# Latent attention in another order of query blocks: 7, 0, 6, 1, 5, 2, 4, 3 in place of 7 down to 0

## The reference, cut to what matters

```
logits = q_h . k_lat * 256**-0.5   (+ a large negative number where hidden)
p      = softmax(logits)           over keys of blocks 0..i for query block i
o_h    = p . (k_lat[64:] w_uv_h)   the values of each head, made before
```

## Time and profile before

| | |
|---|---|
| time, median of 3 runs | 2830.73 us (2829.38 to 2832.75) |
| the profiled execution's own time, and its span | 2828.45 us, 2826.6 us |
| TensorE busy over the span | 2685.5 us (95%) |
| VectorE, ScalarE, GpSimd busy | 1899.6 (67%), 1090.0 (39%), 1674.9 us (59%) |
| latent attention, first score product to the last weighted values | 1793.3 to 2091.1 us |

### The profile page before, as it was taken

How to read it: one execution, slowest core, us unless ns; L and a number is a source line. 1 busy time by engine, 2 the same in 40 slices (tenths; PEclk the granted TensorE clock), 3 DMA queues, 4 the chain that set the end, 5 groups by cost and what they waited for, 6 DMA issues and landing times.

```text
span 2826.6 us, 42358 instructions
## 1 busy us (share of the span) xinstructions
PE 2685.5 (95%) x15781; PEld 1357.9 (48%) x16048; DVE 1899.6 (67%) x2637; ACT 1090.0 (39%) x1665; POOL 1674.9 (59%) x916
## 2 busy tenths in 40 slices
PE   7999888999999999999899999888999999999998
PEld 4666554454444444444444444455554444444443
DVE  6888778575666674256999999777747656664043
ACT  3566566243333200014554343677743433331000
POOL 4777656336677679845348777711113566675884
PEclk9999999999999999999999999999999999999999
DMA  4122455631111153332213222598873111113332
GB/s 150 50 64 72 95 117 120 192 119 54 60 54 55 63 179 127 105 132 82 53 38 149 104 82 97 126 193 193 193 216 130 68 60 60 60 54 126 127 105 97
DMA packets 312622, 297.98 MB, mean 105 GB/s; under 512 B 252720, under 2 KB 252848, under 8 KB 312480
## 3 DMA queue, kind: packets, MB, share of 16 engines
q1 hardware_dynamic: 300672, 272.05, 33.6%
q10 hardware_dynamic: 11808, 23.99, 2.6%
HBM read 189.51 MB, written 35.70 MB: 80 GB/s over the span
## 4 chain that ended last, share of the span: by engine, by line
PE 78%; DVE 6%; issue 4%; DMA 4%; ACT 3%; POOL 2%; ACTq 1%; DVEq 0%; POOLq 0%; SPq 0%
PE ps L1684 23%; PE ps L327 20%; PE ps L309 14%; PE ps L2501 4%; DMA pt<-split 4%; PE ps L643 4%; PE ps L392 4%; PE ps L913 2%; PE ps L2012 2%; PE ps L649 1%; PE ps L2056 1%; DVE split L841 1%; PE ps L884 1%; PE ps L2518 1%; DVE prob L1028 1%
## 5 line engine op out<-in xcount | busy, mean ns | idle before, releaser
L266 POOL TENSOR_TENSOR w_hi<-w_stage,ones 128x1024 bf16<-128x1024 f32 (+1 forms) x115 | 237.6, 2066 | 139.7 <-PE ps L327 85.3
L269 POOL TENSOR_TENSOR w_lo<-w_stage,w_hi 128x1024 bf16<-128x1024 f32 (+1 forms) x115 | 266.5, 2317 | 9.0
L1501 DVE SCALAR_TENSOR_TENSOR x_res<-x_res,ps 128x1024 f32<-128x1024 f32 x32 | 39.0, 1218 | 319.6 <-PE ps L327 318.8
L327 PE MATMUL ps<-w_hi,hid_hi 128*128 128x512 bf16 x689 | 206.3, 379 | 1.6 <-POOL w_lo L269 0.8
L327 PE MATMUL ps<-w_hi,hid_lo 128*128 128x512 bf16 x690 | 206.5, 379 | 0.7
L327 PE MATMUL ps<-w_lo,hid_hi 128*128 128x512 bf16 x690 | 206.5, 379 | 0.7
L2501 PE MATMUL ps<-lat_hi,q_now 128*128 128x512 bf16 (+3 forms) x737 | 186.3, 325 | 5.5 <-DVE row_max L2566 5.5
L309 PE MATMUL ps<-xt_hi,w_hi 128*128 128x512 bf16 x598 | 178.8, 379 | 3.1 <-DVE score L2171 2.5
L309 PE MATMUL ps<-xt_hi,w_lo 128*128 128x512 bf16 x596 | 178.3, 379 | 0.6
L309 PE MATMUL ps<-xt_lo,w_hi 128*128 128x512 bf16 x592 | 177.6, 379 | 0.8
L1684 PE MATMUL ps<-xt_lo,w_hi 128*128 128x512 bf16 x426 | 161.6, 379 | 0.5
(11 more groups left out here) (305 smaller groups left out, 7513.8 us busy)
## 6 DMA issues: line engine op xcount, KB each, us to landing
w_stage<-in_l_up SPq DMA_DIRECT2D x88, 512.0 KB, 3.8
w_stage<-in_l_down SPq DMA_DIRECT2D x88, 512.0 KB, 3.7
w_stage<-in_l_o SPq DMA_DIRECT2D x32, 512.0 KB, 5.9
w_stage<-in_l_q SPq DMA_DIRECT2D x32, 512.0 KB, 5.4
q_split<-q_out SPq DMA_DIRECT2D x32, 512.0 KB, 2.6
q_now<-q_split SPq DMA_DIRECT2D x16, 1024.0 KB, 5.4
w_stage<-in_l_qkv SPq DMA_DIRECT2D x24, 512.0 KB, 4.1
x_spilled<-x_res ACTq DMA_DIRECT2D x16, 512.0 KB, 2.6
```

The costliest lines, as they stand in the source:

```text
L266: pool.tensor_tensor(hi, w_stage[slot][:, 0:cols], ones[:, 0:1].to_broadcast([P, cols]), ALU.mult).then_inc(w_cast[slot], 1)
L269: pool.tensor_tensor(lo, w_stage[slot][:, 0:cols], hi, ALU.subtract).then_inc(w_split[slot], 1)
L327: mm = pe.matmul(ps[:, bank + h, :], a[:, k, rows], w[:, h * HALF:(h + 1) * HALF], start=(k == first and m == 0), stop=(k == tiles - 1 and ...
```

## The change

`latent_block(t)` takes the place of `query_block(t)` everywhere in this stage. A head's steps then have 8, 1, 7, 2, 6, 3, 5 and 4 key blocks. The lags, the waits, the buffers, the number of instructions and the elements that each handles stay. A group of four steps now holds blocks 7, 0, 6, 1 or 5, 2, 4, 3, so that the reciprocal, the scaling and the context's parts address two runs of two blocks in place of one run of four. The pair's two query loads stay ahead of steps 6 and 14, which are now steps of 5 key blocks, followed by one of 4 (before: of 2, followed by one of 1).

```diff
+LATENT_ORDER = (7, 0, 6, 1, 5, 2, 4, 3)
+
+
+def latent_block(t):
+    return LATENT_ORDER[t % TB]
...
-            i = query_block(t)
+            i = latent_block(t)
             pair = split7[t % 4][:, 0:i + 1, :, :]
...
-            cols = slice(HALF, SEQ) if t == 11 else slice(0, HALF)
-            return xt_hi[:, pair, cols], xt_lo[:, pair, cols], ps[:, quad_bank(t), :]
+            twos, _ = quad(t)
+            hi, lo = [x[:, pair, :].rearrange("p (a n) -> p a n", a=4)[:, twos, :] for x in (xt_hi, xt_lo)]
+            return hi, lo, ps[:, quad_bank(t), :].rearrange("p (a n) -> p a n", a=2)
...
-            i = query_block(t)
-            return slice(i, i + 4), t // 8
+            first, second = sorted({latent_block(t - n) // 2 for n in range(4)})
+            return slice(first, second + 1, second - first), t // 8
+
+        def in_twos(ap):
+
+            return ap.rearrange("p (a b) -> p a b", b=2)
...
-                    t, i, hh = slot, query_block(slot), slot // 8
+                    t, i, hh = slot, latent_block(slot), slot // 8
...
-                    blocks, _ = quad(t)
+                    blocks = sorted(latent_block(t - n) for n in range(4))
                     pe.wait_ge(t_cx, 4 * p + t // 4 + 1)
-                    for q, b in enumerate(range(blocks.start, blocks.stop)):
+                    for q, b in enumerate(blocks):
...
-                    blocks, hh = quad(t)
+                    twos, hh = quad(t)
+                    inverse = in_twos(inv7[:, hh, :])[:, twos, :]
                     dve.wait_ge(t_pv, STEPS * p + t + 1)
-                    dve.reciprocal(inv7[:, hh, blocks], sum7[:, hh, blocks]).then_inc(t_ri, 1)
+                    dve.reciprocal(inverse, in_twos(sum7[:, hh, :])[:, twos, :]).then_inc(t_ri, 1)
...
-                m = query_block(t) + 1
+                m = latent_block(t) + 1
                 wait_if(sp, t_pv, STEPS * pair + t - 3)
```

More of the change, by code:

```diff
@@ L2505, in latent_tensor @@
                 if t is not None:
-                    i, hh = query_block(t), t // 8
+                    i, hh = latent_block(t), t // 8
                     if prev is None and t == 0:
@@ L2561, in latent_vector @@
                 if kind:
-                    t, i = slot, query_block(slot)
+                    t, i = slot, latent_block(slot)
                     n = span[i]
@@ L2579, in latent_vector @@
                     dve.wait_ge(t_ri, 4 * p + t // 4 + 1)
-                    dve.tensor_tensor(ctx[:, blocks, hh * 64:(hh + 1) * 64],
-                                      ps[:, quad_bank(t), blocks.start * 64:blocks.stop * 64].rearrange("p (b n) -> p b n", b=4),
-                                      inv7[:, hh, blocks].unsqueeze(2).to_broadcast([P, 4, 64]),
+                    dve.tensor_tensor(ctx[:, :, hh * 64:(hh + 1) * 64].rearrange("p (a b) n -> p a b n", b=2)[:, twos, :, :],
+                                      ps[:, quad_bank(t), :].rearrange("p (a b n) -> p a b n", a=4, b=2)[:, twos, :, :],
+                                      inverse.unsqueeze(3).to_broadcast([P, 2, 2, 64]),
                                       ALU.mult).then_inc(t_cx, 1)
```

## The result

| | before | after |
|---|---|---|
| time, median of 20 runs each, in turns on the same chip | 2829.97 us | 2834.2 us (2831.38 to 2839.18) |
| ratio, 95% interval | | 1.0018 (1.0013 to 1.0024), or +5.1 us (+3.7 to +6.8) |
| span of the profiled execution | 2826.6 us | 2831.2 us |
| busy in it: TensorE, VectorE, ScalarE, GpSimd | 2685.5, 1899.6, 1090.0, 1674.9 us | 2679.3, 1900.2, 1087.6, 1668.7 us |
| latent attention, first score product to last weighted values | 1793.3 to 2091.1 us | 1794.9 to 2095.7 us |

Forecast were 2833 us and no change by more than 0.2%; it came out 0.18% slower, just inside that bound. The interval excludes zero, so it is a small loss. Nothing was gained from the stall that the order was to fill.

The account below looks back on a forecast made before the run. It took a closed round of waits between engines, 17.70 us a head, to bound the kernel. Steady heads +0.6, start +1.0 and end +1.3 gave +2.9 us: no change, 2833 us, range 2826 to 2842.

Parts of the forecast that it names:

- The lane: Maximum, exponential, high part, split and maximum two steps on form one chain; steps 8, 7, 6, 5 share it, 17.14 us a head.
- My walk: Following the program's waits step after step with the prediction's prices; over the old order it gives 17.70 us a head.
- The long round over the load: Round over two heads through the lane, query load and turn of 5: 35.3 us, 17.65 a head, 17.74 with GpSimd's copies.
- GpSimd's copies: Copies of the values fall on the split of 7 once in the long round, adding 0.2 us.
- The gain that was to come: Big turns no longer land in a row, so TensorE's stall before the values of 8, 7 and 6 goes.
- The lost balance (first rival): Lane doesn't bind and balance pays: 2789 us at TensorE's 15.1 a head, or 2824 at the bare lane; chance 0.11.
- The dearer load (second rival): Query load holds the queue 4.4 us or delays the turn of 4: 18.1 a head, 2839 to 2842 us; chance 0.22.
- The lower clock (third): TensorE's clock falls in longer waits, one of about 1.5 us a head: 27 us in 16 heads, 2858 us; chance 0.05.
- The sum: Steady heads +0.6, start +1.0 and end +1.3 make +2.9 us.
- first four heads: Start of the stage: early weights splits share a lane with the longest exponentials, +1.0 us (-1 to +3).
- steady heads: Fourteen steady heads at 17.74 in place of 17.70 us: +0.6 us.
- last head and end: 27 blocks of values left after the last scores in place of 21, last turns of 5 and 4: +1.3 us (0 to +3).

Follow-up runs that it names:

- Small loads: Query loads of all later pairs cut to 16 KB: on the changed kernel 2827.22 us, ratio 0.9994; on the old order 2828.14 us, 0.9995.
- the pair of lags: Against the kernel before: split three steps back, new order 0.9971, old order 1.0061; values alone six steps back, new order 1.0016, old order 0.9968.
- second profile: The changed kernel profiled once more, nothing altered: 2833.54 us, span 2831.7 us, steady heads 17.74 us.
- old order with the split three back: Order 7 down to 0 with lags 3, 6, 7, 8 in place of 2, 5, 6, 7: 2848.45 us, ratio 1.0061 against the kernel before.
- with both in order: Changed kernel with order 0, 7, 6, 1, 3, 5, 4, 2 and query load ahead of the turn of 1: 2807.24 us, ratio 0.9921 against the kernel before.
- order 7, 0, 1, 6, 5, 2, 3, 4: Changed kernel with this block order, lanes of 8, 2, 6, 4 and 1, 7, 3, 5: 2826.05 us, ratio 0.9992 against the kernel before.

## Why the prediction was right, point by point

**The lane: right, and 0.24 short.** It was put at 17.14; the rows give 5.02 + 4.53 + 4.05 + 3.78 = 17.38. The term that was too small is the last, 3.55 for the step of 5. The next step of 8 can't take its maximum when the split of 5 two slots before it is done (idle 0.19 above). Its scores reuse the banks of the step of 5, so they start when the maximum of 5 ends (0.82 + 0.07), and need 2.91 to their own maximum: 3.80. My walk had this wait in its order of events, the sum of four prices did not. Small loads show the lane alone, 17.40 and 17.57. That the lane binds is shown by the pair of lags that moves the two orders in opposite directions.

**The long round over the load: right.** 35.3 forecast, 35.34 in the heads shown; others take 35.4 to 35.6 and one 36.2. The mean of steady heads, 17.74 forecast, was 17.83 in one profile and 17.74 in the other. The load costs 17.83 - 17.49 = 0.34 (or 0.25) a head against a lane without it. Without the load the order gains 0.2 a head on the old one (17.49 against 17.67), too little for the medians to show it (2827.22 and 2828.14).

**What makes some of these rounds longer** is the landing of the turn of 5 behind the load. In rounds that start with a head of 17.40 this turn is issued after 20.47 to 20.52 and lands after 26.80 in the one shown, after 26.79 to 27.01 in most others. The two heads end 8.53 or 8.54 later in every one: 35.34 after a landing at 26.80, 35.51 after 26.97, 35.55 after 27.01. In the longest, 36.22, the turn (issued at 1911.02) landed after 27.69 (source view):

```profile
DMA to landing us min/median/max: 7.2/7.2/7.2
```

So the term that varies is the time for which the load holds up this turn. By the sum of the prediction, 3.7 for a landing at 26.65, it is 3.85 in the round shown, up to 4.06 in most and 4.74 in the longest; why it varies is open. The 35.34 so close to 35.3 is in part luck: the landing came 0.15 later than in the walk, and what follows it took 0.1 less.

SyncE is held up behind the load too. Its turn of 4 behind the load and the turn of 5:

```profile
1949.19 3.22 SPq L2619 DMA_TRANSPOSE pt<-split  x1
```

SyncE holds on to this one issue for 3.22 us (2.2 to 3.5 in the heads that I read), 1.23 in the kernel with small loads. The split of 8 that follows ends at 1952.17 and its turn is issued at 1952.51, 0.34 later, when SyncE is free; the walk allows 0.07. By the prediction the load held up landings only. It does not lengthen these heads: the values of that step of 8 then wait 0.07. Why SyncE stays so long was not tried apart from the load's length. The 0.2 that I had added for GpSimd's copies did not occur: splits of 7 take 1.09 on the mean from 1900 to 2060, the copies beside them or not. So the bare walk (17.65) fits the heads shown, and the later landings take the place of the copies.

**The gain that was to come:** the stall before 8, 7 and 6 did shrink, as forecast. The values of 8 and 7 waited 0.89 and 0.78 for their landings; in the steady heads after, they wait 0.06 to 0.32 and 0.12 to 0.49, those of 6 hardly at all, and those of 5 wait 1.2 to 2.6 instead. Both rounds that replace the old one are as long as it was.

**The lost balance (first rival) fell:** no steady head is shorter than 17.39. Its own condition does not decide it by itself: the split of 8 starts 3.87 after its maximum (1933.54 - 1929.67; 3.88 in the other steady heads), and it was to be less than 3.88, which is just the sum of the lane's prices. **The dearer load (second rival) fell** in most rounds, with 3.85 to 4.06 against the 4.1 from which it was to decide; in one round of each profile it held, the one of 36.22 and one of 35.90 in the second profile, 18.1 and 17.95 a head. **The lower clock (third) fell** in this kernel: windows of the after kernel around the longest wait shown,

```profile
1952.00:1954.00 2.00, 0.57 (x16) 0.40 (x15) 1.93 (x8) 0.86 (x2) 0.00 (x0) 1.00 1.26 257
1954.00:1956.00 2.00, 1.95 (x20) 1.23 (x17) 1.18 (x3) 1.91 (x5) 0.00 (x0) 1.00 1.13 217
```

TensorE was busy 0.57 of 2 us, and its clock was 1.00 (2.4 GHz) then and after. The fall in the earlier trace rows came after 0.52 of 2 us, so that one number was no guide. The Trainium skill, "TensorE: Matmul & The Clock Gate", section "HAM oscillation", describes a kernel whose waits for a transfer, of about 3 to 5 us, bring a fall at every tile. The prediction left out that length: the waits at the values of 5 are shorter here, 1.2 to 2.6 us, and no steady head of this kernel shows a fall. The old order with the split three back does, though none of its waits for a landing is longer than 1.4 us from 1900 to 2060, so the length of the longest wait is no guide either.

**The sum: right in all, not in its parts.** Span of the profile, in us:

| part | forecast | profile after | second profile |
|---|---|---|---|
| stage begins later (code ahead of it unchanged) | 0 | +1.5 | +2.8 |
| first four heads | +1.0 | +1.6 | +1.7 |
| steady heads (fourteen in the forecast, eleven here) | +0.6 | +1.5 | +0.4 |
| last head and end | +1.3 | 0.0 | +0.1 |
| sum, of spans | +2.9 | +4.6 | +5.1 |

The end came out at nothing, and the clock hides what I had put there. From the last step of 8 to the last values it takes 27.03, before 27.01. But before, TensorE's clock fell in the last head; in the two profiles after it did not, and with small loads (the last head has no load in any of them) it fell again. Windows of before, after and the new order with small loads:

```profile
2085.00:2089.00 4.00, 4.00 (x22) 2.28 (x21) 0.00 (x0) 0.55 (x1) 0.00 (x0) 0.57 0.21 40
```

```profile
2089.00:2093.00 4.00, 3.70 (x42) 2.35 (x43) 1.58 (x4) 1.03 (x2) 0.00 (x0) 1.00 1.10 106
```

```profile
2082.60:2086.60 4.00, 4.00 (x24) 2.22 (x21) 0.82 (x3) 0.21 (x1) 0.00 (x0) 0.57 1.21 146
```

Where the clock fell, the new order takes 28.06 and the old one 27.01 (26.98 and 26.65 in two more profiles): 1.0 to 1.4 more, about the +1.3 of the forecast. In the old order the last values, of 1, start at 26.77, though their turn landed at 24.21 (from the start of the last head): TensorE, busy 4.00 of 4 us at the lower clock, comes late to them. How often the clock falls there in the timed runs is not known.

The start can't be settled: over the profiles of all these kernels the stage begins between 1793.3 and 1796.6, and the first four heads of the old order with its own lags took 75.7 to 78.4 (split lag 2, values 5). The +1.6 lies within that, and in the second profile the +1.7 has a fall of the clock in the third head in it. That a later start and an end without a fall cancel is luck. Of the loss of 4 to 5 us, 0.4 to 1.5 lies in the steady heads; where the rest comes from is open.

## What to carry to other kernels

With a fixed order of slots on each engine, write down which steps hang on one another at a distance of the lag, and sum the big ones of each such lane: an alternation of big and small steps puts all big ones into one lane when the lag is even. Balance the lanes as well as the neighbours, and look which turn stands behind a large load in the same queue; the same idea was worth -0.8% with both in order and +0.18% without. A round that hides under another one of nearly its length pays nothing when only one of the two is shortened.

## What the runs showed of the hardware

- The transposing transfer of a step of 4, behind a load of 1024 KB and the turn of 5, keeps SyncE for 2.2 to 3.5 us with its issue, 1.2 without the load; what SyncE issues next can be late by that. A turn of 1 behind the load and a turn of 2, in the kernel before, keeps it for 1.2.
- Where a weights split of VectorE and a copy of GpSimd overlap in the heads read, the one that begins second takes longer. In the order 7, 0, 1, 6, 5, 2, 3, 4 a split of 7 that began 0.12 after a copy (1934.39 and 1934.28) took 1.44 in place of 1.09 us. In the change a copy that began 0.27 after a split of 7 (1938.48 and 1938.21) took 1.29 in place of 0.62, and the split stayed at 1.09.
- TensorE's clock stayed at 1.00 after a wait of 2.6 us for one landing in the change, and fell (0.57 over 4 us) after several waits of at most 1.4 us in the old order with the split three back.
- The first head of the changed kernel took 22.59 us in one execution and 20.72 in the other, while the means of their steady heads differ by 0.1. The clock fell in both (0.81 and 0.76 over 4 us each in the one, 0.86 and 0.71 in the other), so it doesn't tell them apart.
